# Second block without the meta tokens' queries and rows: four tiles from the first real token

## The reference, cut to what matters

```python
def second_block(x, meta_tokens, ...):
    h = jnp.concatenate([meta, x], axis=1)              # 16 + 512 rows
    h = h + mixer(rmsnorm(h, g), ..., pos, topk)
    u = rmsnorm(h, g2).reshape(b * t, d)
    h = h + hier_moe(u, ...).reshape(b, t, d)
    return rmsnorm(h, norm_final_g)[:, N_META:]
```

## Time and profile before

| what | us |
|---|---|
| median of 3 runs | 2379.25 |
| the profiled execution | 2376.9 |
| its span, first to last instruction | 2374.5 |

### The profile page before, as it was taken

How to read it: one execution, slowest core, us unless ns; L and a number is a source line. 1 busy time by engine, 2 the same in 40 slices (tenths; PEclk the granted TensorE clock), 3 DMA queues, 4 the chain that set the end, 5 groups by cost and what they waited for, 6 DMA issues and landing times.

```text
span 2374.5 us, 26276 instructions
## 1 busy us (share of the span) xinstructions
PE 2208.1 (93%) x10155; PEld 1504.0 (63%) x10155; DVE 1001.7 (42%) x2012; ACT 445.5 (19%) x837; POOL 102.6 (4%) x136
## 2 busy tenths in 40 slices
PE   8999999999989999999999999999999987777886
PEld 6888888445657888887847886557875432222232
DVE  6454534124776645443532237867541400000014
ACT  2010100145362101000121114551122000000002
POOL 0000000000001000000110000210000000000000
PEclk9999999999999999999999999999999999889898
DMA  4132222311023223232124121001251899999996
GB/s 158 54 107 71 89 82 78 103 36 36 1 90 107 73 71 107 71 111 80 50 72 98 41 80 49 5 16 54 80 185 59 328 426 427 426 427 427 426 385 282
DMA packets 173002, 348.35 MB, mean 147 GB/s; under 512 B 18148, under 2 KB 143204, under 8 KB 152418
## 3 DMA queue, kind: packets, MB, share of 16 engines
q1 hardware_dynamic: 166752, 332.05, 37.7%
q0 software_dynamic: 5536, 12.71, 1.5%
q10 hardware_dynamic: 610, 2.17, 0.2%
HBM read 337.47 MB, written 16.45 MB: 149 GB/s over the span
## 4 chain that ended last, share of the span: by engine, by line
PE 70%; DMA 16%; DVE 6%; issue 3%; ACT 2%; DVEq 1%; SPq 1%; ACTq 0%; POOL 0%; POOLq 0%
PE PS L608 19%; DMA M<-w 11%; PE PS L639 10%; PE PS L3468 7%; PE PS L72 7%; PE PS L2807 5%; DMA M<-w_ffn_up 4%; PE PS L2992 2%; PE PS L388 2%; PE PS L972 2%; PE PS L1546 1%; PE PS L1898 1%; PE PS L942 1%; PE PS L999 1%; DMA M<-expert_rows 1%
## 5 line engine op out<-in xcount | busy, mean ns | idle before, releaser
L608 PE MATMUL PS<-M 128*128 128x256 f32 x2464 | 537.1, 380 | 4.7 <-DMA M<-w_ffn_up 3.3
L608 PEld LDWEIGHTS PS<-M 128*128 128x128 f32 x2464 | 466.5, 190 | 76.0 <-DMA M<-w_ffn_up 10.3
L3468 PE MATMUL PS<-M 128*64 128x512 f32 x1536 | 362.1, 630 | 85.1 <-DMA M<-w 62.0
L3468 PEld LDWEIGHTS PS<-M 128*64 128x64 f32 x1536 | 113.2, 145 | 321.5 <-issue 217.6
L639 PE MATMUL PS<-M 128*128 128x256 f32 x1232 | 268.7, 379 | 4.7 <-DVE M L731 2.5
L639 PEld LDWEIGHTS PS<-M 128*128 128x128 f32 x1232 | 233.6, 190 | 41.5 <-issue 10.2
L3557 DVE TENSOR_TENSOR M<-M,PS 128x512 f32<-128x512 f32 x16 | 11.0, 687 | 411.4 <-PE PS L3468 411.4
L734 DVE TENSOR_TENSOR M<-M,PS 128x256 f32<-128x256 f32 x220 | 92.6, 421 | 200.1 <-PE PS L608 195.7
L72 PE MATMUL PS<-M 128*128 128x264 f32 (+1 forms) x710 | 168.8, 398 | 2.9 <-ACT M L1708 1.3
L72 PEld LDWEIGHTS PS<-M 128*128 128x128 f32 x710 | 133.4, 190 | 33.4 <-issue 6.9
L2807 PE MATMUL PS<-M 128*128 128x264 f32 x616 | 138.8, 387 | 3.3 <-DVE M L2906 1.8
(11 more groups left out here) (413 smaller groups left out, 2309.3 us busy)
## 6 DMA issues: line engine op xcount, KB each, us to landing
M<-w SPq DMA_DIRECT2D x128, 1024.0 KB, 18.5
M<-w SPq DMA_DIRECT2D x32, 2048.0 KB, 23.0
M<-w_ffn_gate SPq DMA_DIRECT2D x22, 1024.0 KB, 5.5
M<-w_ffn_up SPq DMA_DIRECT2D x22, 1024.0 KB, 5.4
M<-w_ffn_down SPq DMA_DIRECT2D x16, 1024.0 KB, 5.0
M<-w_in SPq DMA_DIRECT2D x13, 1024.0 KB, 5.3
M<-w_in SPq DMA_DIRECT2D x25, 512.0 KB, 3.9
M<-w_ffn_down SPq DMA_DIRECT2D x8, 768.0 KB, 4.4
```

Of the source, the lines that this page charges most:

```text
L608: last = nc.tensor.matmul(PS[:, 3 * half + BANK[p], 0:HALF], lhs[:, a, :], rhs[:, a, :], start=p in FIRST and a == 0, stop=p in LAST and a ...
L3468: last = nc.tensor.matmul(PS[ROWS * k:ROWS * k + ROWS, bank, :], wide[:, a * P + ROWS * k:a * P + ROWS * k + ROWS], weights(k), start=star ...
```

## The change

The meta tokens still give keys and values (and so stay in the norms, ka, va, ckv, krope and ki). Their queries, gates, output rows, routing, expert rows and final rows are no longer computed. The query tiles and row tiles are now four, from row 16 on. The qb, qi and qa tiles are single matmuls of 512 columns (`G1`); the gates' token halves are 256 wide; the fifth part of the first attention has 240 queries and a diagonal of 112; the masks take 7 transfers. `keep_busy`, the planner's times and steps, the choice tiles, and all of the experts' matmuls are as before.

```diff
+OUT_TILES = [(META + P * t, P) for t in range(4)]
+NT = len(OUT_TILES)
-SPILL = (2 * S2 - EXPERTS) // ROWS
+SPILL = (2 * S1 - EXPERTS) // ROWS
...
-                    last = G2.matmul(nc, PS, 2 * (n % 2), w[:, a, :], xnT[:, a, :], a == 0, a == KD - 1)
+                    if n < 8:
+                        last = G1.matmul(nc, PS, 2 * (n % 2), w[:, a, :], xnT[:, a, META:S2], a == 0, a == KD - 1)
+                    else:
+                        last = G2.matmul(nc, PS, 2 * (n % 2), w[:, a, :], xnT[:, a, :], a == 0, a == KD - 1)
...
+                G, lo = (G2, 0) if n % 2 else (G1, META)
                 for a in range(KD):
-                    last = G2.matmul(nc, PS, head_bank(n), slot(s, 0, KD, P)[:, a, :], xnT[:, a, :], a == 0, a == KD - 1)
+                    last = G.matmul(nc, PS, head_bank(n), slot(s, 0, KD, P)[:, a, :], xnT[:, a, lo:S2], a == 0, a == KD - 1)
...
-        PARTS = {1: (0, 384, 144), 2: (1, 256, 272), 3: (2, 128, 400), 4: (3, 256, 272), 5: (4, 0, 256)}
+        PARTS = {1: (0, 384, 144), 2: (1, 256, 272), 3: (2, 128, 400), 4: (3, 256, 272), 5: (4, META, 256 - META)}
-        STEPS, EG = 21, S2 // 2
+        STEPS, EG = 21, S1 // 2
...
-                if s < 3:
-                    sp.dma_start(MB[UNCUT:P, s, 0:KEYS[s] - UNCUT + 16], CHOSEN[s][0:head, 0:KEYS[s] - UNCUT + 16]
-                                 ).then_inc(masks_in, 16)
-                    sp.dma_start(MB[0:UNCUT, s + 1, 0:KEYS[s]], CHOSEN[s][head:P]).then_inc(masks_in, 16)
-                else:
-                    sp.dma_start(MB[UNCUT:P, s, :], CHOSEN[s][0:head]).then_inc(tail_masks_in, 16)
-                    for m in range(4):
-                        sp.dma_start(MB[32 * m:32 * m + 32, 4, :], CHOSEN[s][32:64]).then_inc(tail_masks_in, 16)
+                seen_keys = META + P * (s + 1)
+                sp.dma_start(MB[64:P, s, 0:seen_keys], CHOSEN[s][0:64, 0:seen_keys]
+                             ).then_inc(masks_in if s < 3 else tail_masks_in, 16)
+                if s < 3:
+                    sp.dma_start(MB[0:64, s + 1, 0:KEYS[s]], CHOSEN[s][64:P]).then_inc(masks_in, 16)
...
-        E_UNITS = [(j, h) for j in range(4) for h in range(8)] + [(4, 0), (4, 1)]
+        E_UNITS = [(j, h) for j in range(NT) for h in range(8)]
...
-                if n == LAST:
-                    values(n - 1)
-                    turn_meta(j)
-                    values(n)
-                    values_meta(j)
-            turn_out()
+            values_of_two(LAST - 1)
+            turn_sums(NT - 1)
+            values_meta(NT - 1)
...
+                if n == LAST:
+                    sums_inverted(j)
                 w, bank = P * unit_keys(n), slot_bank(SLOT["p", n])
                 turned(("p", n), PTX[:, n % 3, 0:w], PS[:, bank, 0:w])
-                if h == 7:
+                if h == 7 and n < LAST:
                     sums_inverted(j)
...
-            sums_inverted(4)
-            dve.drain()
-            out_rows()
-            bank = slot_bank(SLOT["o", 4])
-            turned(("o", 4), YB[:, :, S1:S2],
-                   PS[:, bank, 0:P].rearrange("p (m r) -> p m r", m=4)[:, :, META:2 * META])
+            out_columns(NT - 1)
-        HN2 = S2 // 2
+        HN2 = S1 // 2
...
-                            pe.wait_ge(e_copied, len(SLOT))
+                            pe.wait_ge(e_out, HEADS_BEFORE + NT)
...
-        ORDER = (4, 0, 1, 2, 3)
-        HN_JOBS = [(k, t, half) for k, t in enumerate(ORDER) for half in range(2 if TOK_TILES[t][1] == P else 1)]
+        HN_JOBS = [(t, half) for t in range(NT) for half in range(2)]
...
-            for k in range(1, 6):
-                last = nc.tensor.matmul(PS[:, 0, 32 * k:192], ones, columns[:, 0:192 - 32 * k], start=False, stop=k == 5)
+            for k in range(1, NT + 1):
+                last = nc.tensor.matmul(PS[:, 0, 32 * k:wide], ones, columns[:, 0:wide - 32 * k], start=False, stop=k == NT)
...
-            then(tt(OHG, OHG, bc(C["valid"], 4), ALU.mult))
...
-            for t in range(2, 5):
+            for t in range(2, NT):
                 weighted(t)
                 last_pair(t - 1)
                 normed(t - 2)
-            last_pair(4)
-            normed(3)
-            normed(4)
+            last_pair(NT - 1)
+            normed(NT - 2)
+            normed(NT - 1)
...
-            sp.wait_ge(e_av, 5)
+            sp.wait_ge(e_av, NT)
```

More of the change, by code:

```diff
@@ L2126, in masked, with diagonal @@
             return u > 0 and unit(u)[1] != 4
+        def diagonal(u):
+            return P - META if unit(u)[1] == 5 else P
         sp_masked, a_masked, SP_MASKED0, A_MASKED0 = j_x, j_rot, 2, 2
@@ L2466, in scores_of_two @@
                 j = E_UNITS[2 * p][0]
-                if j < 4:
-                    for part in range(1 if j < 3 else 2):
-                        for n in pair:
-                            h, bank = E_UNITS[n][1], main_bank(n)
-                            rows = slice(64 * (h % 2), 64 * (h % 2) + 64)
-                            q, k = QB[rows, h // 2, j * P:(j + 1) * P], KB[rows, h // 2, :]
-                            if j < 3:
-                                out, keys = PS[:, bank, 0:META + P * (j + 1)], k[:, 0:META + P * (j + 1)]
-                            elif part == 0:
-                                out, keys = PS[:, bank - 1, 512 - META:512], k[:, 0:META]
-                            else:
-                                out, keys = PS[:, bank, :], k[:, META:S2]
-                            last = nc.tensor.matmul(out, q, keys, start=True, stop=True)
-                            if j < 3 or part == 1:
-                                last.then_inc(e_s, 1)
-                    return
@@ L2976, in out_pe, with rows @@
         def out_pe(pe):
[L2977 to L2990 removed]
+            def rows(n, t, half):
+                lo = OUT_TILES[t][0]
                 for a in range(KD):
@@ L3019, in out_pe @@
             pe.wait_ge(wo_in, 16)
-            for n, (k, t, half) in enumerate(HN_JOBS):
-                lo, w = TOK_TILES[t]
+            for n, (t, half) in enumerate(HN_JOBS):
                 pe.wait_ge(hn_free, n + 1)
-                if w < P:
-                    strips(n, lo, w)
-                else:
-                    rows(n, lo, half)
-                if half == 0 and k >= 2:
-                    logits(k - 2)
-                if half == 1:
-                    turn(k - 1)
-            turn(4)
-            logits(3)
-            logits(4)
+                rows(n, t, half)
+                if half == 0 and t >= 2:
+                    logits(t - 2)
+                if half == 1 and t >= 1:
+                    turn(t - 1)
+            turn(NT - 1)
+            logits(NT - 2)
+            logits(NT - 1)
         def out_act(act):
@@ L3056, in out_act, with store @@
+            def store(t):
+                act.wait_ge(un_ready, t + 1)
+                act.dma_start(u_dram[P * t:P * t + P, :], UN[t]).then_inc(u_stored, 16)
+            for n, (t, half) in enumerate(HN_JOBS):
+                act.wait_ge(hn_ready, n + 1)
+                nc.scalar.activation(HN[:, t, 512 * half:512 * half + 512], PS[:, n % 2, :], ACT.Copy).then_inc(hn_free, 1)
+                if half == 0:
+                    if t > 0:
+                        store(t - 1)
                     continue
@@ L3259, in first_best @@
                 then(tt(dest, values, bc(best, n), ALU.is_equal))
-                then(tt(dest, dest, over(order, 5), ALU.mult))
+                then(tt(dest, dest, over(order, NT), ALU.mult))
                 then(nc.vector.reduce_max(place, dest, axis=AX))
@@ L3513, in experts_pe @@
             pe.wait_ge(routing_given, 4)
-            for t, (lo, w) in enumerate(TOK_TILES):
-                dest = PS[:, 7, lo:lo + w] if w == P else PS[:, 4, 0:w]
+            for t in range(NT):
                 for j in range(2):
-                    last = nc.tensor.matmul(dest, LAST_SLOTS[2 * t + j][0:w], ident[0:w, 0:w], start=j == 0, stop=j == 1)
+                    last = nc.tensor.matmul(PS[:, 7, P * t:P * t + P], LAST_SLOTS[2 * t + j], ident, start=j == 0, stop=j == 1)
             last.then_inc(routing_made, 1)
```

427 lines of the change are left out of this document (171 added, 256 removed).

## The result

The changed kernel takes **2354.66 us** (median of 4 runs, 2354.2 to 2356.83), against 2378.18 (4 runs) for the kernel before beside it: ratio 0.9908, 95% interval 0.9896 to 0.9920. That is 23.5 us, where 23.8 was forecast. The total hides a miss: one step went the other way by some 3 us, and other terms and the scatter of the runs made up for it.

A forecast was written before the change was run, and what follows sets the result against it. TensorE was taken to bound the kernel before the experts, and the start of the weight stream within them. Terms summed to 23.8 us, taken from the 2378.3 average to give 2354.5 us; range 2347 to 2363.

The forecast's parts named there:

- Steps 1 to 5: Projections 3.5, first attention 1.0, end of the second attention 4.7, gates 0.3 and 3.4, output stage 5.2 us saved.
- Step 6: Routing: nothing won up to the first product, shorter VectorE operations and fewer records after it; 1.1 us saved.
- Steps 6 and 7: Routing, 1.1 us saved, and experts, 0.3 us saved with 16 pairs kept; everything else shifts with its start.
- Step 8: Last rows: VectorE leads, tile 3 ends the chain instead of the meta tile; 4.3 us saved.
- The selection or the short tail binds: Second attention's end held by POOL's broadcast, or selection takes back gains: 2.2 to 4.3 us lost; chance 0.16.
- The clock helps: The clock's fall at 1844 to 1846, before the routing's filler, moves away: 2351.8 us; chance 0.08.
- The clock hurts: Clock falls to 1.2 GHz in the gates; 112 slow records eat the gain, all 568 give 2475; chance 0.02.
- step 1: Projections: query tiles become 512-column matmuls with half the records, TensorE leading; 3.5 us saved.
- The stream of weights: Expert weights' stream does not start earlier: gains up to 1866 (19.2 us) vanish, 2373.7 us; chance 0.03.
- 16 pairs: Experts: rival that the change doesn't do what it says, with a further pair of experts costing 31 us; chance 0.01.

The follow-up runs named there:

- The repeat: The changed kernel run again with nothing altered, as the base of the next three runs; measured 2355.87 us.

## Why the prediction was right, and where it was not

**Steps 1 to 5** hold nearly to the tenth. Projections: 3.5 forecast, 3.29 in the traces, 3.3 when undone. First attention: 1.0 and 1.14. End of the second attention: 4.7 and 4.73. Gates: 0.3 and 3.4 against 0.21 and 3.74. Output: 5.2 and 5.62. These are stages in which TensorE leads, and each was priced by counting its records from rows of the same kernel; such a count was good to 0.4 us a step.

**Step 6** was wrong twice. First in its size: the gather is issued 24.73 us after the logits begin before the change and 21.89 after, so the chain won 2.8 us and not 1.1. The sentence that failed is that up to the first product "nothing is won", since the filler binds as VectorE does. The repeat shows VectorE setting the product at 7.17 us, with the filler done 1.75 us earlier; before it was 7.9. So 0.7 was won here. Another 0.8 was won in the logits, for which the forecast had no term and which is the clock's (see the rivals); the part behind gave 1.3, near the 1.1 forecast.

**Steps 6 and 7** then failed in their sign. Both took for granted that the experts start when the routing is done. Counted from the start of SP's stream (L3374 before, L3283 after), the gather was issued 19.2 us later before the change and 16.4 after, but its rows landed at 24.2 and 23.5: the stream decides. In the six executions of the changed kernel and its variants in which all of the 8 MB went ahead and the gather followed 16.4 to 17.6 us after their start, the rows landed 23.3 to 23.6 us after it, whenever the gather was issued. The 2.8 us of the chain ran into it, and the idle time that arose took the clock from the first pair. The sentence that failed is that "everything else shifts with its start". The forecast had 1.4 us here; the first profile shows 1.83 lost, 3.2 us apart. With the weights moved the stage does give its gain, 447.4 to 444.9: 2.5 us.

**Step 8**: 4.3 forecast. The rows from the first sum of the last rows to the end take 24.15 us after (2328.95 to 2353.1) and 28.4 before (2346.10 to 2374.5), 4.25 less. In the span it gives 3.77, since the store and load of the expert rows ahead of it took 0.5 more. The last chain is the one forecast, tile 3 in place of the meta tile:

```profile
2343.29 1.22 DVE L3507 TENSOR_TENSOR M<-M,PS 128x1024 f32<-128x1024 f32 x1
...
2348.69 1.28 DVE L3494 SCALAR_TENSOR_TENSOR M<-M 128x1024 f32<-128x1024 f32 x1 [0.66 <-ACT M L3528]
```

**How the total came right.** The profiled executions stand 22.0 us apart: the sum of 23.8, less the miss of 3.2 and 0.5 of step 8, plus 0.6 from steps 1 to 5 together, 0.7 of the first block's scatter and 0.6 outside the span. The medians stand 23.5 apart, because the profiled execution of before was a quick one. That 2354.5 met 2354.66 is partly luck: the loss of 3.2 us is covered by terms that nobody forecast. The mechanism of steps 1 to 5 and 8 is not luck.

**The rivals.** "The selection or the short tail binds": no; undoing step 1 alone gives back its 3.3 us, and the broadcast is hidden. "The clock helps" came true in part: the clock fell later after the change. Before, it is 0.50 from 1844 to 1846, under the last logits, which take 4.57 us; after, it is 0.87 from 1824 to 1826 and the logits take 3.76, and the filler behind them takes 7.11 for 7.83. Why the fall came later is open. "The clock hurts" named the gates as its place, where it did not come; it came in the first pair, after an idle time that no rival foresaw, and costs some 1.4 us, not the gain. What the prediction calls half transposes, the 53 us before the gates, is by its lines (L2508, L2525, L2515, L2518) 20.5 of 55.9 us of TensorE's work, nearer two fifths; no term hangs on it. The stream of weights did start earlier, by 19.5 us, and there are still 16 pairs. By the Trainium skill (DMA: Bandwidth & Descriptors, section "Queues, rings and completion order") the DMA engines take turns between the queues packet by packet, by which a gather of 128 rows need not wait for a stream ahead of it. The table does not bear that out: with about 2 MB of weights in flight the gather takes 6.8 to 8.1 us and with free engines 3.5 to 3.8, so the turns do not save it. The same page's fit for a transfer issued by GpSimd (section "Anatomy of one DMA", 2.0 us plus the bytes at 436 GB/s) would give an estimate of 3.2 us for these 512 KB, near what the free engines show.

## What to carry to other kernels

A change that moves a latency-bound transfer forward in time is to be checked against what lies on the DMA engines at its new time: not only who waits for it, but what was issued ahead of it. Prefetches for later go behind the wait for the small transfer that everybody needs now; here that is one line moved, worth 5 us after the change and nothing that could be measured before it. The best version is the change with that move, 2350.1 us against 2354.7 and 2378. And a time that is met says little: compare the stages, each against its term.

## What was not expected of the hardware

- Idle time of TensorE and the first pair's records go together over fourteen executions: up to 1.17 us of idle the 64 records took 13.95 or 13.96 us (eight executions), from 2.49 us on 15.46 to 16.91 (six executions; in the first of them the granted clock is 0.50 after 1850). But the idle time of 2.1 us ahead of the output stage cost the clock in three executions of twelve, so one profile of such a place is not enough.
- The gather's landing grows with the weights that are still in flight when it is issued (estimates from each stretch's length and GB/s): 3.5 to 3.8 us with none, 5.0 with 0.8 MB, 5.8 with 1.6, 6.8 to 7.2 with 2.1, and 8.1 with 2.1 issued together with it. How much had been issued in all says less.
- TensorE's time at the start of a stage that is bound by DMA counts, where buffers come free by it. From 1882 to 2235 the page of the changed kernel has 426 to 428 GB/s in every slice; with the weights moved the first pair ends 6.6 us sooner after the logits (42.7 for 49.3), and 4.4 of it are left at the last pair.
